# A hybrid decoder layer on eight cores: w_up cast into a DRAM scratch ahead of time, the last tile's second norm on VectorE, and FFN state terms at another place

## The reference

```python
h = rmsnorm(x, g_pre_mix);  z = h @ w_in          # u, v, bg, cg, ga, gb
a, new_pool = multiscale_pool(u, ...)             # trailing means, small matmul
cv, new_conv = causal_dwconv(cg * v, buf_conv, w_conv)
b = (bg * cv) @ w_conv_out
merged = sigmoid(ga) * a + sigmoid(gb) * b
x = x + rmsnorm(merged @ w_o, g_post_mix)
h = rmsnorm(x, g_pre_ffn)                         # the "second norm" of a tile
upc, new_ffn = causal_dwconv(h @ w_up, buf_ffn, w_ffn_conv)   # 2*2816 channels
gate, val = split(upc)
y = (silu(gate) * val) @ w_down
x = x + rmsnorm(y, g_post_ffn)
```

## Time and profile before

| | before |
|---|---|
| time, median of 3 runs | 834.52 us (834.33 to 835.03) |
| time of the profiled execution | 834.0 us |
| its span on core 7, first to last instruction | 832.4 us |
| spans of the other cores | 825.7 to 832.1 us |
| busy: PE, VectorE, ScalarE, GpSimd | 801.2, 556.6, 471.8, 269.0 us |
| granted TensorE clock, mean of the span on core 7 | 0.989 |

### The profile page before, as it was taken

The page is one execution under the profiler, slowest core; times in us unless marked ns, Lnnn a source line. Parts: engine busy times, 40 slices in busy tenths (PEclk is TensorE's granted clock), DMA queues, the critical chain, the costliest instruction groups (busy, mean ns, idle before and its releaser), DMA issues.

```text
span 832.4 us, 16714 instructions; the slowest of 8 cores (825.7 to 832.4 us)
## 1 busy us (share of the span) xinstructions
PE 801.2 (96%) x5108; PEld 499.1 (60%) x5108; DVE 556.6 (67%) x1046; ACT 471.8 (57%) x923; POOL 269.0 (32%) x305
## 2 busy tenths in 40 slices
PE   6999999999999999989969999999999999999994
PEld 4455455555555555556646666666666666666662
DVE  2987438876957686578756586658656766685723
ACT  3433386676575646687834475557555654775531
POOL 6432002001002262589662243225212522152231
PEclk9999999999999999999989999999999999999998
DMA  9999706556116999999990033004201500050073
GB/s 171 199 152 157 158 1 154 144 128 140 55 36 155 128 152 196 176 153 168 174 152 1 2 67 37 26 24 62 55 1 35 70 1 1 2 69 2 2 124 82
DMA packets 62838, 75.16 MB, mean 90 GB/s; under 512 B 3072, under 2 KB 59264, under 8 KB 62736
## 3 DMA queue, kind: packets, MB, share of 16 engines
q0 software_dynamic: 41440, 44.97, 39.4%
q1 hardware_dynamic: 21312, 29.14, 13.1%
HBM read 81.53 MB, written 22.90 MB: 125 GB/s over the span
## 4 chain that ended last, share of the span: by engine, by line
PE 88%; DMA 5%; ACT 2%; issue 2%; POOL 2%; DVE 1%; DVEq 0%; ACTq 0%; POOLq 0%; SPq 0%
PE ps L464 88%; DMA big<-xT 2%; DMA h2T<-big 1%; DMA big<-w_up 1%; DVE big L821 1%; POOL big L835 1%; POOL big L477 0%; POOL big L757 0%; ACT big L817 0%; DVEq L1047 0%; DVE big L865 0%; ACT big L941 0%; ACT big L834 0%; ACT big L724 0%; ACT big L848 0%
## 5 line engine op out<-in xcount | busy, mean ns | idle before, releaser
L464 PE MATMUL ps<-big 128*128 128x346 bf16 (+4 forms) x5108 | 801.2, 320 | 19.7 <-ACT big L845 6.5
L464 PEld LDWEIGHTS ps<-big 128*128 128x128 bf16 x5108 | 499.1, 99 | 321.5 <-issue 26.4
L821 DVE SCALAR_TENSOR_TENSOR big<-ps,big 128x344 f32<-128x344 f32 (+1 forms) x528 | 280.4, 569 | 108.5 <-ACT big L817 90.0
L835 POOL TENSOR_TENSOR big<-big 128x344 bf16<-128x344 f32 x132 | 124.9, 949 | 256.5 <-DVE big L821 176.1
L817 ACT ACTIVATE big<-ps,big 128x344 f32<-128x344 f32 (+1 forms) x264 | 138.6, 542 | 65.7 <-PE ps L464 61.2
L834 ACT ACTIVATE big<-big 128x344 f32<-128x344 f32 x132 | 64.3, 489 | 38.5 <-DVE big L821 36.8
L475 POOL DMA_DIRECT2D big<-xT x16 | 15.6, 1011 | 174.7 <-DVE big L707 107.8
L694 ACT ACTIVATE big<-ps 128x392 f32<-128x392 f32 (+1 forms) x80 | 39.0, 514 | 53.4 <-PE ps L464 32.2
L845 ACT ACTIVATE big<-ps,big 128x344 f32<-128x344 f32 x48 | 26.0, 547 | 57.9 <-PE ps L464 55.7
L707 DVE SCALAR_TENSOR_TENSOR big<-ps,big 128x392 f32<-128x392 f32 (+1 forms) x40 | 25.8, 646 | 41.8 <-PE ps L464 41.0
L477 POOL DMA_DIRECT2D big<-w_up x44 | 33.4, 764 | 53.2 <-PE ps L464 47.6
(11 more groups left out here) (62 smaller groups left out, 375.6 us busy)
## 6 DMA issues: line engine op xcount, KB each, us to landing
big<-w_up POOLq DMA_DIRECT2D x44, 256.0 KB, 13.1
big<-w_in POOLq DMA_DIRECT2D x32, 256.0 KB, 24.2
yT<-big POOLq DMA_DIRECT2D x21, 344.0 KB, 6.5
big<-xT POOLq DMA_DIRECT2D x16, 392.0 KB, 8.5
yT<-big SPq DMA_DIRECT2D x8, 784.0 KB, 8.7
big<-w_dn POOLq DMA_DIRECT2D x8, 704.0 KB, 20.1
big<-xT SPq DMA_DIRECT2D x6, 784.0 KB, 6.0
big<-h2T SPq DMA_DIRECT2D x6, 692.0 KB, 6.3
```

What stands on the lines that cost most here:

```text
L464: ins = e.matmul(o, lhsT=l, rhs=x, start=(start and i == 0), stop=(stop and i == last))
L821: dve(lambda e, b=b, fj=fj, tt=tt, k=k: e.scalar_tensor_tensor(out=tt[:, 0:n], in0=ps[:, b * 512 + k:b * 512 + k + n], scalar=cc(C_WF + 44 ...
L835: S.add("pool", lambda e: e.tensor_tensor(out=gb.ap[:, j, :], in0=g, in1=v, op=ALU.mult), [T.t()], [gb.t(j, 1)], dur=NB * 2.17 + 100)
```

## The change

1. **w_up.** A new DRAM tensor `wu16` holds w_up as bf16. `wcast` casts one block after another from w_up into wu16 by GpSimd's queue: 8 under `B` of tile 1, 18 each under tiles 2 and 3. `wup`, at the places where it stood (but two blocks rather than one in each round of `B` of tile 4), now loads blocks from wu16 by SP's queue, without a cast.
2. **Tile 4's second norm.** `epi_x` of tile 4 becomes what it is for the others: one instruction per channel block on VectorE, with a priority that draws it forward. The sums of `epi_n2` may be placed 2500 instead of 6000 ns (of the scheduler's clock) behind their inputs.
3. **FFN state terms.** `pre_ffn` (load of st_ffn, three GpSimd operations) stands behind tile 3's `B` rather than at the start of FFN tile 1; its buffer moves from Y's place to that of h2b.
4. **Scheduler.** When the next instruction on an engine would change ScalarE's table, one of the present table that becomes ready within 400 ns goes first.

```diff
                     c = min((x for x in a if ready[x.idx] <= s), key=lambda x: x.pri + x.off + (SWITCH if x.tab not in (None, tab) else 0.0) - (DMAEARLY if x.dma and e == "pool" else 0.0))
+                    if c.tab not in (None, tab):
+                        near = [x for x in a if x.tab == tab and ready[x.idx] <= s + 400.0]
+                        if near:
+                            c = min(near, key=lambda x: x.pri + x.off)
+                            s = max(s, ready[c.idx])
...
+    wu16 = nc.dram_tensor("wu16", [128, 44 * KC * 128], BF16).ap()
...
-    ST_FFN = Buf(Y.off, 44, 2 * NS)
+    ST_FFN = Buf(h2b.off, 44, 2 * NS)
...
             dst = Buf(W_UP.b[i].off, 1, (k - i) * BL, True)
-            pool_dma(dst.flat, w_up[:, i * BL:k * BL], [], [dst.t()], 128 * (k - i) * BL * 4, mx=2048,
+            sp_dma(dst.flat, wu16[:, i * BL:k * BL], [("wu", b) for b in range(i, k)], [dst.t()],
+                   128 * (k - i) * BL * 2, after=[last_pe[0]])
+            i = k
+
+    cast_next = [0]
+
+    def wcast(n):
+        for _ in range(n):
+            i = cast_next[0]
+            cast_next[0] += 1
+            pool_dma(wu16[:, i * BL:(i + 1) * BL], w_up[:, i * BL:(i + 1) * BL], [], [("wu", i)], 128 * BL * 4, mx=2048,
                      after=[last_pe[0]])
...
     def epi_n2(t):
-        rstd(XSQ2[t], 0 if t == NTA - 1 else 2, TA[t], lo_of(t, LO), flt=6000.0 if t == NTA - 1 else 4000.0)
+        rstd(XSQ2[t], 0 if t == NTA - 1 else 2, TA[t], lo_of(t, LO), flt=2500.0 if t == NTA - 1 else 4000.0)
...
-        if last:
-            act(lambda e: e.activation(out=r, in_=r, func=AF.Copy, scale=cc(C_G3 + k)),
-                [R[t].t(k, 1), KCST, ("y", t, k // 4)], [R[t].t(k, 1)], N, ap=1)
-            pool_tt(lambda e: e.tensor_tensor(out=h, in0=r, in1=SD.ap[:, rs, lo:N], op=ALU.mult),
-                    [R[t].t(k, 1), SD.t(rs, 1)], [H2S[t].t(k, 1)], N)
-        else:
...
+        dve(lambda e: e.scalar_tensor_tensor(out=h, in0=r, scalar=cc(C_G3 + k), in1=SD.ap[:, rs, lo:N],
+                                             op0=ALU.mult, op1=ALU.mult),
+            [R[t].t(k, 1), SD.t(rs, 1), KCST], [H2S[t].t(k, 1)], N, stt=True, pri=-30000 + 1500 * k if last else 0)
...
-            if t == NTA - 1:
-                wup(1)
+            if t == L:
+                wup(2)
+            elif t > 0:
+                wcast(1)
...
         for i in range(16):
             F_block(t, i)
+            if i % 2:
+                wcast(1)
         load_x(t + 1, 2)
         prenorm(t + 1)
         WO(t - 1)
+        wcast(2)
         epi(t - 1)
         B(t)
+        if t == 3:
+            pre_ffn()
```

More of the change, by code:

```diff
@@ L425, in build_nc @@
     H2, G = [h2a, h2b], [g0, g1]
-    ST_FFN = Buf(Y.off, 44, 2 * NS)
-    assert ST_FFN.end <= Y.end
+    ST_FFN = Buf(h2b.off, 44, 2 * NS)
+    assert ST_FFN.end <= PRE.off and R[1].end <= ST_FFN.off + 1600
     TAIL = Buf(h2a.off, 1, 44 * 18)
@@ L495, in wup @@
             dst = Buf(W_UP.b[i].off, 1, (k - i) * BL, True)
-            pool_dma(dst.flat, w_up[:, i * BL:k * BL], [], [dst.t()], 128 * (k - i) * BL * 4, mx=2048,
+            sp_dma(dst.flat, wu16[:, i * BL:k * BL], [("wu", b) for b in range(i, k)], [dst.t()],
[7 more added lines that the diff above has]
+            pool_dma(wu16[:, i * BL:(i + 1) * BL], w_up[:, i * BL:(i + 1) * BL], [], [("wu", i)], 128 * BL * 4, mx=2048,
                      after=[last_pe[0]])
-            i = k
     def load_x(t, parts, after=()):
@@ L776, in epi_x @@
         r, h = R[t].ap[:, k, lo:N], H2S[t].ap[:, k, lo:N]
-        if last:
-            act(lambda e: e.activation(out=r, in_=r, func=AF.Copy, scale=cc(C_G3 + k)),
-                [R[t].t(k, 1), KCST, ("y", t, k // 4)], [R[t].t(k, 1)], N, ap=1)
-            pool_tt(lambda e: e.tensor_tensor(out=h, in0=r, in1=SD.ap[:, rs, lo:N], op=ALU.mult),
-                    [R[t].t(k, 1), SD.t(rs, 1)], [H2S[t].t(k, 1)], N)
-        else:
-            dve(lambda e: e.scalar_tensor_tensor(out=h, in0=r, scalar=cc(C_G3 + k), in1=SD.ap[:, rs, lo:N],
-                                                 op0=ALU.mult, op1=ALU.mult),
-                [R[t].t(k, 1), SD.t(rs, 1), KCST], [H2S[t].t(k, 1)], N, stt=True)
+        dve(lambda e: e.scalar_tensor_tensor(out=h, in0=r, scalar=cc(C_G3 + k), in1=SD.ap[:, rs, lo:N],
+                                             op0=ALU.mult, op1=ALU.mult),
+            [R[t].t(k, 1), SD.t(rs, 1), KCST], [H2S[t].t(k, 1)], N, stt=True, pri=-30000 + 1500 * k if last else 0)
         if k % 4 == 3:
@@ L953, in build_nc @@
         F_block(t, i)
+    L = NTA - 1
     def B(t):
@@ L970, in epi @@
             epi_x(t, k)
-    L = NTA - 1
     B(0)
@@ L985, in build_nc @@
         WO(t - 1)
+        wcast(2)
         epi(t - 1)
         B(t)
+        if t == 3:
+            pre_ffn()
+    assert cast_next[0] == 44
     for i in range(16):
@@ L1012, in build_nc @@
         if t == 1:
-            pre_ffn()
             assert up_next[0] == 44
```

## The result

The changed kernel takes 844.3 us (median, 843.9 to 845.6) beside 834.8 us for the one before in the same runs: a ratio of 1.0114, 95% interval 1.0097 to 1.0132. It is slower by 1.1%, where 1.3% faster was forecast. The profiled execution is that of core 6, span 842.4 us; the other cores take 833.7 to 840.4.

A forecast was written before the change was run, and what follows sets the result against it. PE bounds the kernel, busy 801 of 832 us, so only its gaps count. Core 2, slowest at 822.0 after its gains, plus 1.6 around the span, 0.5 for VectorE, -0.3 for tables gives 823.8 us; range 822.0 to 828.5.

The forecast's parts named there:

- the one on the casts: Stage A, tiles 1 to 3: 84 us of cast traffic, DMA share near 0.95, hidden by PE's work; cost 0.
- The casts hurt tiles 1 to 3 (slower, 838): Late accumulating loads of x delay norm sums of tiles 0 to 2 some 5 us each; 15 us lost, 838 us, 5%.
- the gap behind L845: PE's wait behind the weight stage for the first wdown eviction: 6.5 us plus 2.2 us of lower clock, all gone.
- the sum: Core 7's gains: 6.5 and 2.2 for the wdown eviction, 1.6 for w_up, 0.5 for L726; 10.8 us in all.
- the w_up wait: PE's wait for a w_up block behind the weight stage, 1.6 us on core 7, 2.2 on core 2, to go.
- 12 us of margin: Slack claimed for tile 4's h2 store, most of it from emptied queues, as argument against the store staying late.
- the rival on the store: Tile 4's h2 store stays late, having taken 12.47 us on core 7 with the cast queue full; 829 us, 7%.
- the clock of 1.00 between 430 and 445 us: Sign of being right: PE's granted clock full behind the former wdown gap, where it had been 0.65.
- spans within some 2 us of each other: Sign of being right: all cores' spans differ by no more than some 2 us.
- sums of a norm before 335 us: Sign of being wrong: PE waiting for norm sums in stage A, before 335 us.
- VectorE or GpSimd late: Tile 4's second norm: GpSimd 3 us late, or VectorE's products blocked by GpSimd's, makes PE wait; 826.5 us, 15%.
- The state terms: Moved behind tile 3's cast, three GpSimd operations and the st_ffn load cost nothing; uncovered, 4 to 5 us on GpSimd alone.

The follow-up runs named there:

- e6: Changed kernel with 22 whole casts at every second place, the other 22 w_up blocks loaded directly by cast loads: 824.67 us, 0.993 of before.
- e7: Changed kernel with w_up loaded directly and, in place of the casts, unread plain float32 DRAM copies by SP's queue: 883.08 us, 1.0629 of before.
- e8: Changed kernel without scratch or casts (e1), with the sums of tile 4's second norm 24 matmuls later on PE: 824.37 us, 0.9927 of before.
- e5: Changed kernel with only the first 4 of 44 casts, all w_up loads reading those blocks, output not the layer's: 823.69 us, 0.9927 of before.
- e1: Changed kernel without its scratch: no casts, w_up loaded by casting loads as before, all else as changed: 829.97 us, 0.9938 of before.
- e2: Kernel before with the scratch alone: casts under tiles 1 to 3, w_up loaded by SP: 850.76 us, 1.019 of before.
- e12: Changed kernel with 4 whole casts and 40 of an eighth of a block, output not the layer's: 825.38 us, 0.9939 of before.
- e9: Changed kernel, all 44 casts, with the second norm's sums of tiles 0 to 3 placed later on PE: 833.16 us, 1.0047 of before.
- e4: Changed kernel with its 44 casts moved: 16 under B of tile 0, 14 each under F_block of tiles 2 and 3: 839.38 us, 1.0047 of before.

## Why the prediction was wrong

**The step that failed** is the one on the casts: "The stretch from 256 to 335 us had a share of 1.01 with the same kind of casts under it and PE did not wait once; I take 0." The amount was about right: 84 us of engine time on 59, "a share near 0.95", measured 0.98. The inference was wrong. A share says that engines are busy, not how far the queues lag, and of the accumulating loads of x only tile 3's fall whole in the stretch that I took as proof; tile 2's stand at its edge (253.6 to 258.8 us) and landed in 7.1 us. Tile 3's loads showed the lag. The kernel before, tile 1's four loads, then tile 3's:

```profile
L475 POOL DMA_DIRECT2D big<-xT x4: 850/856/890, 192.9 to 198.1; - x4
...
DMA to landing us min/median/max: 5.3/7.1/7.4
```

```profile
L475 POOL DMA_DIRECT2D big<-xT x4: 875/1034/1186, 298.1 to 307.1; - x4
...
DMA to landing us min/median/max: 9.1/11.6/13.0
```

11.6 us where tiles 1 and 2 have 7.1, at the share that was forecast for the casts: ScalarE waited 1.8 us for it and PE not at all. With 44 casts all eight 20-us slices from 145 to 305 us have a share of 1.06 to 1.27, and tiles 1 and 2 get their loads after 22.2 and 15.1 us. High slices alone don't do it: e6 has 1.17 and 1.05 from 145 to 185 us, but its tile 1's loads, issued behind these, land in 7.2. I had also averaged: the mean of 0.39 over 151 us hid that 125 to 205 us of the kernel before already stood at 0.50 to 0.68, just where tiles 0 and 1 have their accumulating loads (issued 134.6 to 139.4 and 192.9 to 198.1), and there the casts were put.

**The rival** "The casts hurt tiles 1 to 3 (slower, 838)" is what took place, by its mechanism: sums of norms at fixed places on PE, late loads of x. It was given 5%, its price was 15 us; stage A lost 22.4. Two things were missing in it. Tile 1's and 2's loads took 15 and 8 us longer than before, not 5, though some of that was borne; tile 0's took 10.4 us instead of 8.6 (the longest 17.1 instead of 11.5), and tile 3's only 9.2 instead of 11.6. And nearly each gap draws a lower clock behind it, some 8 us together, which I had priced for the gap behind L845 (2.2 us) and not here. Its doubt, that the loads share the casts' queue, is at most a part of it: e7 shows them late with no cast in that queue. The Trainium skill (DMA: Bandwidth & Descriptors, Issuing engines are not separate DMA queues) says that DMAs of all issuing engines run on the same 16 DMA engines and interleave. The 14.2 us of e7 agree.

**What went as forecast.** Behind stage A the sum was 10.8 us, less 0.5 for VectorE and plus 0.3 for tables: 10.6; measured 12.4. The sum had left out PE's small waits for taps there, 0.24 to 0.54 us each, which went too. The whole gap of L845 and its low clock went, the w_up wait went (here and, without bare loads, in e8). Exp of the first norm ended 13.4 us behind the first w_up matmul, the last sum 40.6, the four products 57.8; I had 16.7, 45.2 and 61.7, if counted from 339.3. I had counted from 343.0, the row behind a gap, not from the first w_up matmul, which is the constant error of some 4 us in these. Tile 4's first h2T store went out at 419.65, 58.0 us behind; the second half, which the sum had not separated, only at 437.27, and no wait came of it. The "12 us of margin" of the rival on the store do not follow from the sum: 417.4 - 401.5 - 12.47 leaves 3.4 us. No run shows the 829 of that rival: the stores cost PE nothing here. A lower clock behind such a gap was not sure either: in the kernel before core 2 stayed at 1.00 behind 3.77 us of idle, while core 6 of the change fell to 0.50 behind 2.80.

Of the signs that were named, the clock of 1.00 between 430 and 445 us came; spans within some 2 us of each other did not (833.7 to 842.4), and sums of a norm before 335 us, a sign of being wrong, did. Nothing came of "VectorE or GpSimd late": PE ran 461 us without a wait, the four products took 2.23 us; GpSimd had no product beside them, so the contention of that rival was not tried. The state terms cost nothing that shows: e5 has them too, from 185.8 us on, and PE busy for 151.00 of 151 us. In e5, where casts cost little, the time was 823.69 us against a forecast of 823.8, but the kernel before took 830.3 in that group; the ratio, 0.9927, is the fairer figure, and 0.987 had been forecast.

**What is shown and what is open.** Shown: the loss is that of the casts (e1, e2, e5), of their size and not their number (e12), and it comes with the second half of them (e6). That it reaches PE through ScalarE's waits for accumulating loads is read from the chain and the timeline above; e9 confirms it for the sums, somewhat over a third of the casts' cost. Open: how much of it is order within GpSimd's queue and how much the engines as such, since e7 differs in bytes too; what the cores do to each other, since all eight cast in every run; why tile 3's sums wait in e5 and e12 as well; and whether 44 casts spread evenly over all of stage A could be hidden. e4, the one other spread that was tried, could not.

## What to carry to other kernels

Background traffic is not free because PE is busy elsewhere: before it is costed at nothing, find the small transfers with a deadline in the same stretch, read their landing times slice by slice, and see what they are when the queues are full. A mean DMA share over a long stretch hides the places where the deadline lies. And see first what a prefetch can win at most: here the change with all but free casts (e5) was no faster than the same change without a scratch and with a later place for one norm's sums (e8), 0.9927 both.

## What was not expected of the hardware

The DMA share of a 20-us slice went up to 1.27, so it is no share of a fixed whole: the packets' times that are summed in it must overlap. A cast from DRAM to DRAM took about the engine time of a casting load (q0: 39.7% of 842.4 us with the scratch, 39.4% of 832.4 before, both 44.97 MB), while a plain float32 copy of a block took (25.8% of 879.3 - 12.5% of 827.8) / 44 = 2.8 us on all engines, against 1.9 us estimated for a cast.
